# Sums of squares on four column groups of TensorE, added by a second product: a diffusion block on eight cores

## The reference

```python
def rmsnorm(x, g):
    xf = x.astype(jnp.float32)
    y = xf * lax.rsqrt(jnp.mean(xf * xf, axis=-1, keepdims=True) + EPS)
    return (y * g.astype(jnp.float32)).astype(x.dtype)
...
def block(x, mods, s0_f, s0_b, rows, norm_ffn1, ...):
    m = lambda i: mods[:, i, None, :]
    h = rmsnorm(x, norm_ffn1) * (1.0 + m(1)) + m(0)
    x = x + 0.5 * m(2) * swiglu(h, w1_ffn1, w3_ffn1, w2_ffn1)
    h = rmsnorm(x, norm_mix) * (1.0 + m(4)) + m(3)
    mix, s_f, s_b = mixer(h, w_in, w_decay, b_decay, gla_norm, conv_w, w_out, s0_f, s0_b, rows)
    x = x + m(5) * mix
    h = rmsnorm(x, norm_ffn2) * (1.0 + m(7)) + m(6)
    x = x + 0.5 * m(8) * swiglu(h, w1_ffn2, w3_ffn2, w2_ffn2)
    return x, s_f, s_b
```

## Time and profile before

| what | value |
|---|---|
| time, median of 3 runs | 1321.99 us (1321.18 to 1323.16) |
| profiled execution, its own time | 1323.23 us |
| its span on the slowest core (core 4) | 1321.6 us |
| spans of the eight cores | 1310.7 to 1321.6 us |
| PE busy on core 4 | 1249.8 us, 95% |
| DVE, ACT, POOL busy | 521.6, 399.9, 178.8 us |
| products with ones, 512 wide | 136, of about 0.38 us each |

### The profile page before, as it was taken

One profiled execution on the slowest core, in us unless ns is written; L12 is line 12 of the kernel. 1 busy time (PEld: TensorE's weight loads), 2 busy tenths in 40 slices (PEclk: granted clock), 3 DMA queues, 4 the chain that ended last, 5 costly groups with the idle time before them and its releaser, 6 DMA issues.

```text
span 1321.6 us, 19020 instructions; the slowest of 8 cores (1310.7 to 1321.6 us)
## 1 busy us (share of the span) xinstructions
PE 1249.8 (95%) x6648; PEld 573.2 (43%) x6648; DVE 521.6 (39%) x804; ACT 399.9 (30%) x647; POOL 178.8 (14%) x298
## 2 busy tenths in 40 slices
PE   2679999999999999989999999999999999999996
PEld 1234444444444444344444444444444444444444
DVE  2124134211233244466467667521243112432456
ACT  3265100111100245577545336621100111001344
POOL 3013100110001010110434322300001000000000
PEclk9989999999999999999999999999999999999999
DMA  9981734647734211010412322812313221020123
GB/s 176 220 195 33 128 58 71 96 65 115 111 62 69 53 68 53 0 33 0 97 18 51 94 70 59 137 23 45 57 28 59 38 32 33 1 48 1 64 64 128
DMA packets 35084, 91.05 MB, mean 69 GB/s; under 512 B 4016, under 2 KB 10672, under 8 KB 32816
## 3 DMA queue, kind: packets, MB, share of 16 engines
q0 software_dynamic: 21888, 62.11, 28.7%
q1 hardware_dynamic: 13104, 27.73, 6.3%
HBM read 137.24 MB, written 14.68 MB: 115 GB/s over the span
## 4 chain that ended last, share of the span: by engine, by line
PE 87%; DMA 5%; DVE 2%; ACT 2%; issue 2%; POOL 1%; DVEq 0%; ACTq 0%; POOLq 0%
PE ps L235 87%; DMA sb_arena<-w_ffn 4%; DVE sb_arena L263 1%; ACT sb_arena L248 1%; DMA sb_arena<-w_ada 1%; DVE sb_arena L252 1%; POOL sb_arena L232 1%; ACT L248 0%; POOL sb_arena L259 0%; PE ps L239 0%; POOL sb_arena L252 0%; DVEq L141 0%; ACTq L141 0%; DVEq L1207 0%; POOL sb_ea L269 0%
## 5 line engine op out<-in xcount | busy, mean ns | idle before, releaser
L235 PE MATMUL ps<-sb_arena 128*128 128x512 bf16 (+4 forms) x5840 | 1198.6, 366 | 25.8 <-DMA sb_arena<-w_ffn 8.3
L235 PEld LDWEIGHTS ps<-sb_arena 128*128 128x128 bf16 (+2 forms) x5840 | 536.7, 98 | 676.9 <-issue 69.9
L248 ACT ACTIVATE sb_arena<-ps 128x512 f32<-128x512 f32 (+3 forms) x281 | 166.1, 599 | 701.4 <-PE ps L235 700.3
L252 DVE TENSOR_TENSOR sb_arena<-sb_arena,ps 128x512 bf16<-128x512 f32 (+1 forms) x208 | 143.0, 688 | 481.1 <-PE ps L235 429.7
L263 DVE SCALAR_TENSOR_TENSOR sb_arena<-ps,sb_der,sb_arena 128x512 f32<-128x512 f32 (+1 forms) x200 | 145.2, 729 | 153.3 <-PE ps L235 153.3
L248 ACT ACTIVATE sb_arena<-sb_arena 128x512 bf16<-128x512 f32 (+4 forms) x193 | 123.5, 660 | 77.8 <-DVE sb_arena L263 63.0
L232 POOL DMA_DIRECT2D sb_arena<-w_ffn x88 | 47.1, 544 | 418.2 <-PE ps L235 388.2
L252 DVE TENSOR_TENSOR sb_arena<-sb_arena 128x512 f32<-128x512 f32 (+1 forms) x98 | 66.2, 717 | 55.1 <-ACT sb_arena L248 54.4
L259 POOL TENSOR_SCALAR sb_arena<-sb_arena,sb_der,sb_modT 128x512 bf16<-128x512 f32 x44 | 40.8, 928 | 267.2 <-DVE sb_arena L252 240.5
L263 DVE SCALAR_TENSOR_TENSOR sb_arena<-sb_arena,sb_vec 128x512 f32<-128x512 f32 (+1 forms) x72 | 53.2, 758 | 23.3 <-ACT sb_arena L248 13.4
L248 ACT ACTIVATE sb_arena<-sb_arena,sb_modT,sb_der 128x512 bf16<-128x512 f32 x48 | 39.0, 813 | 58.7 <-DVE sb_arena L252 44.8
(11 more groups left out here) (39 smaller groups left out, 158.5 us busy)
## 6 DMA issues: line engine op xcount, KB each, us to landing
sb_arena<-w_ffn POOLq DMA_DIRECT2D x44, 512.0 KB, 8.6
sb_arena<-w_ada POOLq DMA_DIRECT2D x36, 512.0 KB, 9.1
sb_arena<-w_ffn POOLq DMA_DIRECT2D x44, 256.0 KB, 9.4
sb_arena<-x SPq DMA_DIRECT2D x8, 1024.0 KB, 12.9
y<-sb_arena SPq DMA_DIRECT2D x24, 256.0 KB, 2.5
xspill<-sb_arena SPq DMA_DIRECT2D x4, 1024.0 KB, 4.0
sb_arena<-xspill SPq DMA_DIRECT2D x4, 1024.0 KB, 6.6
sb_arena<-w_cv POOLq DMA_DIRECT2D x12, 256.0 KB, 7.7
```

The costliest lines, as they stand in the source:

```text
L235: return P.add("pe", lambda e: e.matmul(out, lhsT, rhs, start=start, stop=stop), reads=flat(reads), writes=flat(writes))
L248: return P.add("act", lambda e: e.activation(out=out, in_=in_, func=func, **kw), reads=flat(reads), writes=flat(writes))
L252: return P.add(eng, lambda e: e.tensor_tensor(out=out, in0=in0, in1=in1, op=op), reads=flat(reads), writes=flat(writes))
```

## The change

`norm_slices` gets a second form, used everywhere but for the very first norm (`split=False` there) and `last_half`. `stats4` multiplies piece kc by 128x32 ones into the 32 partitions of column group kc % 4 of bank 7, so that each group of partitions holds the sum over two pieces. ACT copies the bank to bf16 (`hi`), DVE subtracts that from the bank and writes the rest as bf16 (`lo`). An empty slice follows. `combine` multiplies hi and lo by a 128x128 matrix of 1/32 (`c32B`), again into bank 7, which adds the four partial sums, and then does Ln and Exp. hi and lo lie in the space of r. In the wout loop the tick after the first square takes one slice instead of two.

```diff
--- before.py
+++ after.py
@@ -190,6 +190,7 @@
         der = sb("der", [128, 64], F32)
         identB = sb("identB", [128, 128], BF16)
         onesB = sb("onesB", [128, 128], BF16)
+        c32B = sb("c32B", [128, 128], BF16)
         maskFB = sb("mask", [128, 256], F32)
         s0sb = sb("s0sb", [128, 4, 128], F32)
         Wd = sb("Wd", [128, 4, 128], BF16)
@@ -219,6 +220,7 @@
         for t in t_ps:
             t.excl = True
         t_vec, t_id, t_ones, t_mask, t_s0, t_Wd = [Tile(n) for n in ("vec", "id", "ones", "mask", "s0", "Wd")]
+        t_c32 = Tile("c32")
         t_sc, t_rm, t_cst2 = Tile("sc"), Tile("rm"), Tile("c2")
         t_mod = [Tile("mod%d" % i) for i in range(36)]
         t_ea = [Tile("ea%d" % p) for p in range(2)]
@@ -327,7 +329,8 @@
             st[kc] = P.alloc("sq%d" % kc, SQ + kc * KB, KB)
             act(bf(SQ + kc * KB, 512), xv(kc, blk), AF.Square, [t_x[kc][blk]], [st[kc]])
 
-        def norm_slices(blk, apply, done=None):
+        def norm_slices(blk, apply, done=None, split=True):
+
 
 
             sl = nrm["n"] % 2
@@ -350,8 +353,31 @@
             def app(kc):
                 apply(kc, f32(RSTD + sl * 2 * KB, 512), st["r"])
 
+            def stats4():
+                for kc in range(8):
+                    g = kc % 4
+                    mm(ps[g * 32:(g + 1) * 32, 7, :], onesB[:, 0:32], bf(SQ + kc * KB, 512), kc < 4, kc >= 4,
+                       [t_ones, st["sq"][kc]], [t_ps[7]])
+                o = RSTD + sl * 2 * KB
+                t_hi, t_lo = P.alloc("hi%d" % sl, o, KB), P.alloc("lo%d" % sl, o + KB, KB)
+                st["hl"] = ((bf(o, 512), t_hi), (bf(o + KB, 512), t_lo))
+                cp("act", bf(o, 512), ps[:, 7, :], [t_ps[7]], [t_hi])
+                tt("dve", bf(o + KB, 512), ps[:, 7, :], bf(o, 512), ALU.subtract, [t_ps[7], t_hi], [t_lo])
+
+            def combine():
+                for i, (v, t_v) in enumerate(st["hl"]):
+                    mm(ps[:, 7, :], c32B[:], v, i == 0, i == 1, [t_c32, t_v], [t_ps[7]])
+                r = f32(RSTD + sl * 2 * KB, 512)
+                st["r"] = P.alloc("rstd%d" % sl, RSTD + sl * 2 * KB, 2 * KB)
+                act(r, ps[:, 7, :], AF.Ln, [t_ps[7]], [st["r"]], scale=1.0 / D, bias=EPS)
+                act(r, r, AF.Exp, [st["r"]], [st["r"]], scale=-0.5)
+
             out = []
-            if done is None:
+            if split:
+                if done is None:
+                    out += [(lambda k0=k0: squares(k0, 2)) for k0 in (0, 2, 4, 6)]
+                out += [stats4, lambda: None, combine]
+            elif done is None:
                 out += [(lambda k0=k0: squares(k0, 2)) for k0 in (0, 2, 4, 6)]
                 out += [lambda: stats(0, 4), lambda: stats(4, 4)]
             else:
@@ -475,6 +501,7 @@
             dma("pool", bf(off, 2048), wada_d[i], [], [t], "r%d" % off)
             ada0.append((bf(off, 2048), t))
         memset("dve", onesB[:], 1.0, [t_ones])
+        memset("dve", c32B[:], 1.0 / 32, [t_c32])
         for i in range(3):
             F1.load_pair(i, i)
         for blk, gate in ((1, ada0[7][1]), (2, F1.pair[1][1][1]), (3, F1.pair[2][1][1])):
@@ -493,7 +520,7 @@
             tt("dve", f32(off, 512), xv(kc, 0), r, ALU.mult, [t_x[kc][0], t_r], [t])
             pre[kc] = (f32(off, 512), t)
 
-        for s in norm_slices(0, pre_apply):
+        for s in norm_slices(0, pre_apply, None, False):
             s()
         for j in range(4):
             for m in range(2):
@@ -1109,7 +1136,7 @@
                 if d == 0:
                     tick(1)
                 square(sq, blk, d)
-                tick(2)
+                tick(2 if d else 1)
             later(blk, norm6(blk, sq))
             if i == 1:
                 F2.load_pair(0, 0)
```

## The result

The changed kernel takes 1325.44 us (median), the kernel before 1321.94 us in the same set of runs: a ratio of 1.0022, 95% interval 1.0012 to 1.0031. The ratio leaves out the executions that fell into a slower state of the chip (three of these 22, at 1345 to 1491 us), so it means 2.9 us where the two medians differ by 3.5; either way the kernel is slower, by about what was forecast (2.75 us). The profiled execution took 1325.02 us, its span on the slowest core was 1323.4.

The account below looks back on a forecast made before the run. The prediction took PE's matmul slots and its few waits to bound the kernel. Its terms, with 9.1 us of saved slots set against new waits, summed to +2.75 us, a median of 1324.7 us, range 1315.5 to 1329.

Parts of the forecast that it names:

- The tiled eight: Eight 32-column products of each changed norm: 0.65 us on PE, mode changes included, instead of 1.73 us for full products.
- The chain of 2.4 us: From stats4's issue through hi on ACT and lo on DVE: 2.4 us until combine can go.
- Just hidden: Combine behind one wout unit of 1.73 us would not wait; three norm6 there gain 1.95 us.
- Blocks 2 and 3: In ffn_first, PE waits 1.95 us for h 7 at each block, net +1.30 us, twice: +2.6 us.
- rival 3: More half clock: two cold stretches on the slowest core, 1328.2 us, chance 0.18; against it, DVE bounds behind the 3.7 us idle.
- norm3 of blocks 0, 1, 2: Norms at 469, at 501.6 and of block 2: net +0.75, -2.1 and -0.65 us.
- phase_a(0), the mis-sized term: Block 3's norm3: combine waits for ACT's Exp on bank 7, PE idles 3.7 us, scans start later; +2.9 us.
- Rivals 1 and 2: Late norms all hidden, only slots count: 1312.9 us, chance 0.10; half of the waits do not come: 1317.3 us, chance 0.17.
- nine terms of the sum: Net changes by place, in us: +1.05, +2.6, +0.75, -2.1, -0.65, +2.9, -1.95, +1.05, -0.9; together +2.75.

## Why the prediction was right, and where it wasn't

**The tiled eight.** Forecast 0.65 us with both mode changes; from the end of the slot before (91.00 + 0.22) to the next start it is 0.64, and the kernel without second products confirms 1.08 us saved per norm. Right. The Trainium skill (TensorEngine Tiling (Array Packing), Key Properties) says that a change of mode drains TensorE; the trace agrees in so far as the pair of changes costs 0.1 to 0.2 us over the slots of the products (0.55 or 0.64 us, where two full slots are 0.43).

**The chain of 2.4 us.** Where combine follows at once it starts 2.46 us (70.37 to 72.83) and 2.44 us after stats4. In the wout loop it starts 2.51 us after, 0.23 behind the end of the unit in between (802.84 + 1.73). "Just hidden" was a little off: each of the three gives 0.4 to 0.5 us instead of 0.65.

**Blocks 2 and 3.** The mechanism and the place were right: POOL is late, by 1.67 and 0.16 us instead of 1.95. Five matmuls go, then PE waits for h 5, then for h 7; I had looked at h 7 alone, which comes 14.8 us after combine's end (95.76 to 110.58; forecast 14.63). As each idle also leaves the tail of a record unhidden (0.38 less 0.216, 0.17 us), the two come to 2.2 us, net 1.5 instead of 1.3, as block 3's +1.50 shows. The step that failed here is the clock: I counted no half clock behind a wait of 1.95 us, and it came on six cores at 110 and on two at 135. This is rival 3 in part.

**norm3 of blocks 0, 1, 2.** +1.14, -1.97 and -0.95 against +0.75, -2.1 and -0.65. Right in place and sign; the first wait was 1.62 us and not 1.4, and the third figure is in part clock (about -0.4 at full clock).

**phase_a(0), the mis-sized term.** Combine starts 8.58 us after stats4 (forecast 8.65), with 3.53 us of idle that ACT ends (forecast 3.7). The timeline of all engines has the Exps as written, and the scans at 12.0 us after stats4 (forecast 12.1):

```profile
557.54 1.28 ACT L250 ACT_TABLE_LOAD   x1
558.83 1.47 ACT L250 ACTIVATE sb_arena<-ps,sb_der 128x512 f32<-128x512 f32 x2
...
561.35 1.45 ACT L250 ACTIVATE sb_arena<-ps,sb_der 128x512 f32<-128x512 f32 x2
...
566.36 4.99 DVE L770 TENSOR_TENSOR_SCAN sb_arena<-sb_rmask,sb_arena 128x512 f32<-128x512 bf16 x4
```

From stats4 to the transposes behind the second wait it takes 25.42 us instead of 22.96: +2.46, forecast +2.9. But the stretch behind got 1.69 us back. Before, PE had stood 3.57 us at 575 and ran at half clock behind it, where matmuls were the limit. Now the long idle, and the half clock behind it, lie at 563, where DVE is the limit and PE's clock costs nothing. The eight cores show that: from stats4 to the Wd products at 580 each takes 25.86 or 25.87 us, though behind combine six of them ran at half clock for 2.7 to 6.0 us and two (4 and 7) not at all. The second wait is 1.75 us on this core, and full clock follows it on all eight. I had seen the first half of this (rival 3's "against") and not that the old half clock would go away.

So the sum, +2.75 forecast and +2.97 in the profiles, is closer than its steps: it was 2.15 us too low at blocks 2 and 3 and 2.13 us too high in phase_a(0), and of each 1.7 is clock. That these two misses cancel is luck. The waits themselves came where they were forecast, and nearly at their size. Rivals 1 and 2 are out: both wait chains came. What no run here settles is why a core falls to half clock behind one of two equal waits and not behind the other.

## What to carry to other kernels

- A product that works on the result of another engine's work on the product before it costs its round trip (here 2.4 us), not its slots (0.43 us). Place it where more than that of other matmuls lies between (here one FFN unit of 3.45 us hid it, one wout unit of 1.73 us left 0.23 us of it), and count what stands behind it: its consumers come later by the same amount.
- Split such a change by place. Five of the nine terms of the sum had a plus; leaving the old form there turned +0.2% into -0.4%.
- When a wait is taken out, look first at what its engine does next. Freeing bank 7 took 3.5 us of idle away at one place and gave back 4.9 us at the next.

## What the runs showed that I had not expected

- Half clock (0.51 to 0.58 as the mean from 110.4 to 113.9) on six of eight cores behind a wait of 1.67 us, while two cores stayed at 1.00 behind the same wait.
- The same slot of a program can pay for its half clock or not: 1.7 us where PE is the limit (11.63 against 9.95 us at block 2), nothing where DVE is (25.86 us with it and without it in phase_a(0)).
- ACT's table load waits for what its Ln waits for, so it isn't hidden in the wait: behind combine (509.90 to 510.49) it begins only at 510.69. The Trainium skill (ScalarE: Activation LUTs, What ACT_TABLE_LOAD costs) adds a drain of about 1380 ns to a load of about 1283 ns. The load is 1.28 us here too, but behind the Silu that ends at 503.60 it begins at 503.62 and Ln at 504.91, so no such drain shows; the measurement decides.
